# First mixer's output scaled in PSUM in place, the first two query tiles of cross attention interleaved, one weight split moved to GpSimd

## The reference, cut to what matters

```python
h = h + hybrid_mixer(rmsnorm(h, norm_mix_g[l]), ...)          # ends with y_all @ w_out
h = h + memory_cross_attention(rmsnorm(h, norm_xa_g[l]), mem, norm_mem_g[l], w_q, w_k, w_v, w_o)

def hybrid_mixer(...):
    ...
    y_sb = rmsnorm(o, sb_norm_g)                              # the attention half of the mixer
    return jnp.concatenate([y_ssd, y_sb], axis=-1) @ w_out

def memory_cross_attention(hn, mem, ...):
    q = (hn @ w_q).reshape(b, s, 4, 128)
    logits = einsum("bshd,bmhd->bhsm", q, k) / sqrt(128)
    p = softmax(logits)
    o = einsum("bhsm,bmhd->bshd", p, v)
    return o @ w_o
```

## Time and profile before

| | us |
|---|---|
| median of 3 executions | 2032.93 (2030.28 to 2033.87) |
| the profiled execution | 2030.0 |
| its span in the profile | 2028.0 |
| TensorE busy in the span | 1953.9 (96%) |
| TensorE's mean granted clock, as a share of 2.4 GHz | 0.981 |
| VectorE, ScalarE, GpSimd busy | 1270.3, 839.0, 312.6 |

### The profile page before, as it was taken

The page is one execution under the profiler, slowest core; times in us unless marked ns, Lnnn a source line. Parts: engine busy times, 40 slices in busy tenths (PEclk is TensorE's granted clock), DMA queues, the critical chain, the costliest instruction groups (busy, mean ns, idle before and its releaser), DMA issues.

```text
span 2028.0 us, 29769 instructions
## 1 busy us (share of the span) xinstructions
PE 1953.9 (96%) x12259; PEld 1720.8 (85%) x12259; DVE 1270.3 (63%) x1765; ACT 839.0 (41%) x1140; POOL 312.6 (15%) x254
## 2 busy tenths in 40 slices
PE   8999989999999999999999999999997899999998
PEld 6788866789898897999999999998884578889896
DVE  6668766656574654121668476576797548658575
ACT  4448744533232334223444143244434445234243
POOL 2122241200110140011420000002245120000002
PEclk9999999999999998998999999999998899999999
DMA  9753132599999658610265343342121033344241
GB/s 339 207 123 140 63 89 83 181 353 239 228 240 347 254 136 187 151 54 30 72 162 184 120 148 148 116 156 104 63 86 61 8 109 134 120 147 171 99 181 69
DMA packets 68480, 299.14 MB, mean 148 GB/s; under 512 B 6505, under 2 KB 6633, under 8 KB 48386
## 3 DMA queue, kind: packets, MB, share of 16 engines
q1 hardware_dynamic: 38064, 201.15, 27.5%
q0 software_dynamic: 30128, 96.08, 19.9%
q10 hardware_dynamic: 162, 0.10, 0.0%
HBM read 295.19 MB, written 94.96 MB: 192 GB/s over the span
## 4 chain that ended last, share of the span: by engine, by line
PE 61%; issue 26%; DVE 5%; ACT 3%; POOL 3%; DMA 1%; SPq 0%; POOLq 0%; DVEq 0%; ACTq 0%
PE lin L584 36%; PE lin L2015 7%; PE aux L2015 5%; PE lin L1807 1%; PE aux L1605 1%; PE aux L2853 1%; POOL squares L932 1%; ACT w_hi L491 1%; DMA w_raw<-in_weights 1%; PE lin L1560 1%; POOL w_lo L498 1%; PE lin L2823 1%; PE aux L2837 1%; PE aux L1589 1%; POOL r_t L2440 1%
## 5 line engine op out<-in xcount | busy, mean ns | idle before, releaser
L584 PE MATMUL lin<-x_hi,w_hi 128*128 128x512 f32 (+1 forms) x1128 | 397.2, 352 | 7.7 <-DVE h L689 2.9
L584 PE MATMUL lin<-x_hi,w_lo 128*128 128x512 f32 (+1 forms) x1128 | 396.1, 351 | 0.0
L584 PE MATMUL lin<-x_lo,w_hi 128*128 128x512 f32 (+1 forms) x1128 | 395.6, 351 | 0.0
L498 DVE TENSOR_TENSOR w_lo<-w_raw,w_hi 128x2048 fp32r<-128x2048 f32 (+1 forms) x101 | 228.8, 2265 | 152.6 <-ACT w_hi L491 152.2
L491 ACT ACTIVATE w_hi<-w_raw 128x2048 fp32r<-128x2048 f32 (+1 forms) x112 | 210.3, 1877 | 208.2 <-PE lin L584 193.2
L584 PEld LDWEIGHTS lin<-x_hi,w_hi 128*128 128x128 f32 x1128 | 211.9, 188 | 41.5 <-issue 5.0
L584 PE MATMUL lin<-v_hi,w_hi 128*128 128x264 f32 (+1 forms) x704 | 238.0, 338 | 4.7 <-DVE tmp L2543 3.5
L584 PEld LDWEIGHTS lin<-x_lo,w_hi 128*128 128x128 f32 x1128 | 212.1, 188 | 30.0 <-issue 0.2
L584 PEld LDWEIGHTS lin<-x_hi,w_lo 128*128 128x128 f32 x1128 | 212.0, 188 | 29.7
L584 PE MATMUL lin<-v_hi,w_lo 128*128 128x264 f32 (+1 forms) x704 | 234.6, 333 | 0.0
L584 PE MATMUL lin<-v_lo,w_hi 128*128 128x264 f32 (+1 forms) x704 | 234.2, 333 | 0.0
(11 more groups left out here) (477 smaller groups left out, 4472.5 us busy)
## 6 DMA issues: line engine op xcount, KB each, us to landing
w_raw<-in_weights SPq DMA_DIRECT2D x112, 1024.0 KB, 4.8
w_raw<-in_weights SPq DMA_DIRECT2D x43, 768.0 KB, 6.1
w_sum<-weight_sums SPq DMA_DIRECT2D x43, 768.0 KB, 4.6
weight_sums<-in_weights POOLq DMA_DIRECT2D x4, 5120.0 KB, 49.9
weight_sums<-in_weights POOLq DMA_DIRECT2D x2, 7168.0 KB, 55.9
w_raw<-weight_sums SPq DMA_DIRECT2D x43, 256.0 KB, 6.4
weight_sums<-in_weights POOLq DMA_DIRECT2D x8, 1280.0 KB, 13.8
weight_sums<-weight_sums POOLq DMA_DIRECT2D x8, 1280.0 KB, 12.9
```

Source lines behind the costliest of these rows:

```text
L498: does.tensor_tensor(w_lo[:, s, 0:n], w_raw[:, s, 0:n], w_hi[:, s, 0:n].bitcast(F32), ALU.subtract).then_inc(sem("w_lo_ready"), 1)
L584: last = nc.tensor.matmul(o, a, b, start=(k % (L.kc // k_banks) == 0 and p == 0), stop=((k + 1) % (L.kc // k_banks) == 0 and p == 2))
```

## The change

In the mixer's output stage VectorE now multiplies the PSUM tile by `scale_d` in place, waits for that on its own semaphore (`link`), adds the PSUM tile to `h`, and gives the PSUM bank back (`lin_taken`) after the add and no longer after the multiply; an empty engine instruction then signals `h_added`. The high split of `XQ`'s first unit moves from after tile 4 to after tile 2 on ScalarE, the low split from after tile 5 to after tile 3 on VectorE.

TensorE takes query tiles 0 and 1 together: tile 0 over k = 0 to 6 (each k waiting for its operand), tile 1 over k = 0 to 6, then k = 7 of both. The wait for free PSUM is eased by one (`before - 1`), since the two banks of each slot still held two tiles of the layer before. The square sums, which stood between the two tiles, follow both.

The low split of `XQ`'s second unit leaves VectorE's list, where it stood ahead of the root, and goes to GpSimd after the squares of `l_xa`. VectorE waits for it before it splits `XO`'s first unit.

```diff
 def act_mix_output(act):
     for t in range(KD):
         act.wait_ge(sem("h_added"), base + t + 1)
         act_operand(act, l_xa, t, t % 2)
-        if t == 4:
+        if t == 2:
             next_hi(act, WB, 1, 0)

 def dve_mix_output(dve):
     next_lo(dve, WB, 0, 0)
     dve_root(dve, l_sb)
     for t in range(KD):
         slot, before, n = WB.tile(t // 4, t % 4, 0)
-        ht, out_t = h_tile(t, S1), tmp[:, 2 + t % 2, 0:S1]
+        ht, out_t = h_tile(t, S1), lin[slot][:, t // 2 % 2, 0:S1]
         dve.wait_ge(sem("lin_done"), n + 1)
-        nc.vector.tensor_tensor(out_t, lin[slot][:, t // 2 % 2, 0:S1], scale_d[:, 0:S1], ALU.mult)\
-            .then_inc(sem(f"lin_taken{slot}"), 1)
+        link(dve, nc.vector.tensor_tensor(out_t, out_t, scale_d[:, 0:S1], ALU.mult))
+        nc.vector.tensor_tensor(ht, ht, out_t, ALU.add).then_inc(sem(f"lin_taken{slot}"), 1)
         dve.wait_ge(sem(f"lin_taken{slot}"), before + 1)
-        nc.vector.tensor_tensor(ht, ht, out_t, ALU.add).then_inc(sem("h_added"), 1)
-        dve.wait_ge(sem("h_added"), base + t + 1)
+        nc.vector.engine_nop().then_inc(sem("h_added"), 1)
         if t:
             dve_operand(dve, l_xa, t - 1)
-        if t == 5:
+        if t == 3:
             next_lo(dve, WB, 1, 0)
     dve_operand(dve, l_xa, KD - 1)

 def pe_cross(pe):
+    def first_queries():
+        w = [x[:, w_unit % 2, :].rearrange("p (k n) -> p k n", k=KD) for x in (w_hi, w_lo)]
+        def step(m, k):
+            slot = XQ.tile(0, m, 0)[0]
+            for p, (wp, xp_) in enumerate(((w[0], v_hi), (w[0], v_lo), (w[1], v_hi))):
+                mm = nc.tensor.matmul(lin[slot][:, 0, :], wp[:, k, m * P:m * P + P], xp_[:, k, 0:S1],
+                                      start=(k == 0 and p == 0), stop=(k == KD - 1 and p == 2))
+            return mm
+        pe.wait_ge(sem("w_lo_ready"), w_unit + 1)
+        for m in range(2):
+            slot, before, _ = XQ.tile(0, m, 0)
+            pe.wait_ge(sem(f"lin_taken{slot}"), before - 1)
+            for k in range(KD - 1):
+                if m == 0:
+                    l_xa.wait_operand(pe, k)
+                step(m, k)
+        l_xa.wait_operand(pe, KD - 1)
+        for m in range(2):
+            step(m, KD - 1).then_inc(sem("lin_done"), 1)
     def query(t):
         for k in range(KD):
-            if t == 0:
-                l_xa.wait_operand(pe, k)
     ...
-    query(0)
+    first_queries()
     pe_squares(pe, l_xa)
-    query(1)
     logits(0)
     query(2)

 def dve_cross(dve):
-    next_lo(dve, XQ, 0, 0)
     dve_root(dve, l_xa)
     taken(0)
     taken(1)
     maxima(0)
+    dve.wait_ge(sem("w_lo_ready"), XQ.unit0 + 2)
     next_lo(dve, XQ, 1, 0)

 # gpsimd
     pool_squares(pool, l_xa, l_ssd.idx + 1)
+    next_lo(pool, XQ, 0, 0, nc.gpsimd)
     pool_squares(pool, l_ff, l_ff.idx)
```

## The result

| | before | changed |
|---|---|---|
| median of 20 executions each | 2031.70 us | 2036.26 us |
| lowest to highest | 2024.7 to 2037.5 | 2030.0 to 2047.0 |
| span of the profiled execution | 2028.0 | 2040.0 |

The ratio is 1.0030, with a 95% interval of 1.0018 to 1.0041: slower by 3.7 to 8.3 us; the medians lie 4.6 apart, the means 5.9. The forecast was 2035.0 us, slower by 2.1. The changed kernel's profile is of an execution of 2042.19 us, 5.9 above its median, so that its span is not a typical one.

A forecast was written before the change was run, and what follows sets the result against it. TensorE, busy 1953.9 of 2028.0 us, was taken to bound the kernel. +0.2 us at `logits(0)` plus 1.9 for a clock dip gave +2.1, put on the median 2032.93: 2035.0 us, range 2031.3 to 2038.3.

The forecast's parts named there:

- The root's chain: Between square sums and `logits(0)`: ScalarE's root, VectorE's reciprocal and scaling of query tile 0, no longer hidden, 4.9 us.
- the 2.1: Forecast shift of the whole kernel: +0.2 us at `logits(0)` plus 1.9 us for a clock dip, +2.1 us slower.
- Adds 0.69: Mixer output on VectorE: each add out of PSUM takes 0.69 us, against 1.77 where an add collided with GpSimd before.
- multiply into PSUM 0.69: Mixer output on VectorE: the multiply written to PSUM, shown in no row, taken as 0.69 us.
- the upper bound of 1.77: Upper bound for VectorE's multiply into PSUM, from the longest 128x512 add: 1.77 us each, giving +9.7 us, 2042.6.
- rival 3: Mixer output: the multiply into PSUM costs more, slower by over 4 us; priced at +4.9 us, 2037.8; chance 0.09.
- Waits of 1.4 and 1.75: First query tile: TensorE stands 1.4 and 1.75 us for operands, before k = 5 and k = 6.
- `logits(0)` +0.2 us: `logits(0)` starts at 320.7 against 320.48 before: the 6.3 us won at the front are stood through at the back.
- the dip in the root's wait: TensorE's clock falls to 0.50 in the 4.9 us wait before `logits(0)`, slowing it and query tile 2: 1.9 us.
- The bound of 2.0: Upper bound for the clock dip's cost behind the wait before `logits(0)`: 2.0 us, the price of the old dip.
- Rival 1: The clock falls once more, in the operands' waits of the first query tile: +3.8 us, 2036.7; chance 0.30.
- the end of the wait before the queries: Kernel before: TensorE's 6.3 us wait ahead of the first query tile, said to be released by VectorE's weight split.

The follow-up runs named there:

- in turn: Changed kernel with query tiles in turn again and the square sums between them, all other edits kept: 2025.96 us, ratio 0.9975; repeated: 2027.00 us, 0.9983.
- split back: Changed kernel with the low split of the second query unit back on VectorE ahead of the root: 2034.17 us, ratio 1.0020 to before.
- in turn with the split back: Changed kernel with query tiles in turn again and the second query unit's low split back on VectorE: 2029.38 us, ratio 0.9987 to before.
- interleaved only: Kernel before with only the query tiles' interleaving and its eased PSUM wait; scaling and splits as before: 2039.67 us, ratio 1.0042 to before.
- in turn, strict wait: Changed kernel with query tiles in turn again and the PSUM wait back from `before - 1` to `before`: 2031.09 us, ratio 0.9990 to before.
- not in place: Changed kernel with the scaled tile written to SBUF (`tmp`) again, all else as changed: 2039.05 us, ratio 1.0042 to before.

## Why the prediction came out as it did

**Direction and mechanism: right.** The root's chain, hidden before, is open and takes back what the front gives. That step was shown by undoing it (in turn: M 7.2 to 9.4 us less) and by doing it alone (7.5 more than before).

**What is luck in the number.** 2036.26 lies 1.3 us from the forecast, but the difference, 4.6 by the medians, is more than twice the 2.1. The median I built on, 2032.93 of three executions, is 1.2 us above the 2031.70 of twenty; that hid half of the miss.

**The steps with numbers.** Adds 0.69 (687 ns in the mean of 8), multiply into PSUM 0.69 (692): right, so the upper bound of 1.77 and rival 3 are out. Operands 6 and 7 at 307.8 and 308.5: measured 307.5 and 308.15. Query tiles from 300.2: 299.97. Waits of 1.4 and 1.75: 1.16 and 1.47. Root's chain 4.9: 4.89. `logits(0)` +0.2 us without dips ahead of it: 36.91 became 37.05 and 37.04. GpSimd's split unwaited for: right.

**The term that was mis-sized: the dip in the root's wait.** I took 1.9 us, from the one dip shown. M - L is 7.33 without one; with it, it is 9.34, 9.96, 10.21, 9.11 and 10.16 in the five traces that have it: 1.8 to 2.9, 2.4 in the mean. The bound of 2.0 was no bound: how much of the low clock falls on work and how much on waiting differs from one execution to the next. Behind the start of `logits(0)` the clock is low for 3.9, 5.3, 5.9, 3.4 and 5.7 us in these traces, and the loss is half of that within 0.1. The dip I had read was a single draw.

**The rival that holds in part of the executions.** Rival 1, a dip in the operands' waits as well, had 0.30, as if it were one case or the other. Of seven traces with these two waits unfilled three have it (changed, split back, in turn with the split back) and four have not. It is not a case but a mixture. L reads 39.77 and 38.54 with it in the changed order and 37.05 without, 1.5 to 2.7 us. My point was the value of the likeliest case, 2.1; an estimate of the mean over executions from these readings is 0.1 + 2.4 + 3/7 x 2.1 = 3.4. The measured interval begins at 3.7, so some of the slowdown probably lies elsewhere. One place is seen: the 3.7 to 5.9 us that three of seven interleaved traces lose between 743 and 1037. Whether that belongs to the change is open, and no term of the sum had it.

**What I misread in the trace of before.** I called the weight split the end of the wait before the queries. The list of waits says so the earlier trace rows, but the split ended at 305.83 and the matmul started at 306.53, and the chain in the earlier trace rows leaves out 0.69 between them. In that gap stands one row of VectorE's timeline of before:

```profile
305.74 0.68 DVE L737 TENSOR_TENSOR tmp<-lin,scale_d 128x512 f32<-128x512 f32 x1
```

That multiply gave back tile 6's bank at 306.42; PSUM ended the wait, as two runs bear out: with this wait eased alone TensorE starts right behind the split (*interleaved only*), and with the split early alone it still starts only behind tile 6 (*in turn, strict wait*). It did not spoil the sum, since the change eases that wait too, but I gave `before - 1` no worth, and it is 2.1 us of the best kernel.

**Where the expected gain went.** The edits other than the interleaving win 4.5 us together (in turn): the scaling in place, the early splits with the eased PSUM wait, and GpSimd's split, which shows no part in it. The interleaving gives back 4.6 even without a dip (L 32.43 to 37.05) and 7.2 to 9.4 with dips.

## What to carry to other kernels

Before two matmul tiles are merged to fill an early wait, look at what the second tile was hiding: here it covered a chain of 4.9 us through two other engines, and closing 3.7 us of waiting at the front opened that at the back. A wait on TensorE is to be priced with the clock behind it, as a range taken from several traces. And if a wait's named releaser had ended 0.7 us before the waiter started, look for the second condition; easing that one may be the cheaper edit.

## What the runs showed of the hardware

- With nothing in the program or the neighbouring waits changed, the clock fell in some executions and not in others: with waits of 1.16 and 1.47 us it was 0.50 from 307 on in one trace and 1.00 throughout in another of the same kernel. In the wait of 4.89 us it fell in four of the five traces that leave it unfilled, and in the fifth (*not in place*) 0.4 us behind its end, with TensorE at work again.
- VectorE's multiply with its output in PSUM, on the tile it reads, takes 692 ns in the mean of 8, against 685 into SBUF.
- An add with one input in PSUM and one in SBUF ran at 0.69 us from 0.02 us behind the start of GpSimd's squares, where the same add from SBUF took 1.77. The Trainium skill ("SBUF — State Buffer", section "Who interferes with whom") says that a VectorE instruction with at most one SBUF input, outside the 2-port performance modes, does not contend with GpSimd. This case agrees with it: the eight adds out of PSUM take 687 ns in the mean, against 1316 before.
